# The final norm inside the last expert's block, and the last expert's rows added and stored behind it

## The reference

```
h = h + expert_choice_ffn(rmsnorm(h, ffn_norm))
    aff = softmax(t @ w_router)              # 16 experts
    g, idx = top_k(aff.T, 130)               # each expert takes 130 tokens of a group
    y = (silu(xs @ w_gate) * (xs @ w_up)) @ w_down * g
    out[idx] += y                            # a token may be taken by several experts or by none
h = rmsnorm(h, final_norm)
y = h[:, 16:]                                # without the meta tokens
```

## Time and profile before

| | |
|---|---|
| median of 3 runs | 3084.68 us (3084.18 to 3085.31) |
| the profiled execution's own time | 3086.83 us |
| its span | 3084.8 us |
| TensorE busy (matmuls) | 2849.3 us, 92% |
| VectorE, ScalarE, POOL busy | 1842.3 us (60%), 1484.3 us (48%), 664.6 us (22%) |
| mean granted clock of TensorE | 0.962 |
| moved by DMA | 475.79 MB, 154 GB/s |

### The profile page before, as it was taken

One profiled execution on the slowest core, in us unless ns is written; L12 is line 12 of the kernel. 1 busy time (PEld: TensorE's weight loads), 2 busy tenths in 40 slices (PEclk: granted clock), 3 DMA queues, 4 the chain that ended last, 5 costly groups with the idle time before them and its releaser, 6 DMA issues. The chain is left out here.

```text
span 3084.8 us, 56350 instructions
## 1 busy us (share of the span) xinstructions
PE 2849.3 (92%) x20020; PEld 2636.1 (85%) x20020; DVE 1842.3 (60%) x3159; ACT 1484.3 (48%) x2690; POOL 664.6 (22%) x1233
## 2 busy tenths in 40 slices
PE   8999687999999999999999999999955999999991
PEld 7888576999998888888899999988835999999990
DVE  6887555888887777677333343433354555556544
ACT  4333223888887777677322222321222445544532
POOL 0000000444444333333100000000021333333320
PEclk9999898999999999999999999999977999999995
DMA  6656599022022233442847575456644889888857
GB/s 217 178 170 193 164 285 271 21 70 70 22 52 74 73 89 84 112 115 74 256 122 227 140 213 148 137 172 205 186 139 113 204 204 208 204 200 201 200 112 246
DMA packets 596447, 475.79 MB, mean 154 GB/s; under 512 B 56640, under 2 KB 536560, under 8 KB 596288
## 3 DMA queue, kind: packets, MB, share of 16 engines
q1 hardware_dynamic: 577904, 439.28, 50.6%
q0 software_dynamic: 12288, 34.10, 6.2%
q10 hardware_dynamic: 6096, 0.40, 0.1%
HBM read 320.05 MB, written 153.62 MB: 154 GB/s over the span
## 5 line engine op out<-in xcount | busy, mean ns | idle before, releaser
L1444 DVE TENSOR_REDUCE t_peak<-t_s_ps 128x1 f32<-128x1024 f32 (+2 forms) x276 | 336.6, 1220 | 85.0 <-PE t_s_ps L1257 84.3
L1257 PE MATMUL t_s_ps<-t_k,t_q 96*128 96x512 f32 (+2 forms) x1392 | 380.1, 403 | 7.4 <-ACT t_probs L1360 7.4
L1705 PE MATMUL c_acc<-c_tokens,c_w_hi 128*128 128x260 f32 x2048 | 374.0, 284 | 5.3 <-DVE c_w_lo L1778 4.9
L1466 DVE TENSOR_TENSOR t_pt_lo<-t_tp,t_pt_hi 128x512 fp32r<-128x512 f32 x552 | 336.0, 649 | 32.6 <-ACT t_pt_hi L1390 32.1
L1390 ACT CAST t_pt_hi<-t_tp 128x512 fp32r<-128x512 f32 x552 | 284.6, 564 | 113.7 <-PE t_tp L1287 112.5
L1705 PEld LDWEIGHTS c_acc<-c_tokens,c_w_hi 128*128 128x128 f32 x2048 | 317.5, 189 | 5.6 <-issue 5.6
L1360 ACT ACTIVATE t_probs<-t_s_ps,t_bias 128x1024 f32<-128x1024 f32 (+2 forms) x276 | 308.2, 1117 | 22.8 <-POOL t_bias L1520 8.1
L2270 PE MATMUL e_gu<-e_x_hi,w_hi 128*128 128x260 f32 x1024 | 294.1, 287 | 0.9 <-DVE e_x_lo L2413 0.9
L1257 PEld LDWEIGHTS t_s_ps<-t_k,t_q 96*128 96x128 f32 (+2 forms) x1392 | 245.0, 183 | 53.0 <-issue 8.1
L1705 PE MATMUL c_acc<-c_tokens,c_w_lo 128*128 128x260 f32 x1024 | 290.2, 283 | 0.0
L2270 PE MATMUL e_gu<-e_x_lo,w_hi 128*128 128x260 f32 x1024 | 290.1, 283 | 0.0
(11 more groups left out here) (236 smaller groups left out, 6450.5 us busy)
## 6 DMA issues: line engine op xcount, KB each, us to landing
c_raw<-in_w_in SPq DMA_DIRECT2D x64, 512.0 KB, 5.5
w_raw<-in_w_gate SPq DMA_DIRECT2D x64, 512.0 KB, 6.6
w_raw<-in_w_up SPq DMA_DIRECT2D x64, 512.0 KB, 8.2
w_raw<-in_w_down SPq DMA_DIRECT2D x64, 512.0 KB, 4.6
c_tokens<-o_t SPq DMA_DIRECT2D x32, 520.0 KB, 6.7
c_tokens<-hn_t SPq DMA_DIRECT2D x16, 1040.0 KB, 9.1
r_mt<-mix_t SPq DMA_DIRECT2D x32, 512.0 KB, 5.1
t_k<-mk_t SPq DMA_DIRECT2D x32, 390.0 KB, 6.1
```

The costliest lines, as they stand in the source:

```text
L1257: ins = pe.matmul(s_ps[0:r, n % 2, half * 512:(half + 1) * 512], query(n, a), key(n, c, half * 512, (half + 1) * 512), start=(at == 0), st ...
L1444: dve.tensor_reduce(peak[0:r, b % 2, i:i + 1], s_ps[0:r, n % 2, :], AX_X, ALU.max).then_inc(peak_done, 1)
L1466: dve.tensor_tensor(pt_lo[span], tp[:, f % RING, :].rearrange("p (t n) -> p t n", t=4)[:, :, 0:r], pt_hi[span].bitcast(F32), ALU.subtract) ...
L1705: pe.matmul(acc[:, b, mixer, 0:W], w[:, parity, mixer, k, :], tokens[t % 2][:, part, k, cols], start=(k == 0 and at == 0), stop=(k == DK - ...
```

## The change

`finish` is gone, and its work stands in `experts`.

- **The split of results.** For expert 14 all four quarters are transposed at the beginning of the last expert (`results_alternating`), by turns into `tp` and `dn`, and scaled at once. POOL then scatters each quarter when it is done, not all four at the end.
- **The rows.** SP waits for that scatter and for the last weight slab to be split, then loads the 16 blocks of h into room that the weights no longer need (6 on `w_raw`, 4 on `w_hi`, 3 on `w_lo`) and 3 blocks of its own. The last expert's lists of ScalarE and VectorE are written out by hand (`last_body`): squares (L2469) and products (L2577, in place) stand between the `hidden` and `transposed` steps. The products are on VectorE alone. Roots are made in batches of four. SP stores each block as it is done.
- **The last expert's own rows.** POOL gathers their old values from `h_rows` (L2671). TensorE transposes expert 15's outputs into all eight banks; VectorE makes old + gate x output (L2611), ScalarE squares the 260 rows, VectorE makes the roots and the products (L2616), and POOL, once all 16 stores have landed, writes the rows over those stored (L2679). Row numbers of meta tokens lie beyond the bound and are not written.
- **Elsewhere.** `choose` makes the output row numbers `out_rows` (two small VectorE instructions). The gain is loaded on SP's queue as the first thing in `experts`. The weight tensors are now views of one region, at the same sizes. The bodies of experts 0 to 14 are the same but for the order of two waits on POOL.

```diff
-def choose(nc, io, scr, rows_t, gates_t, w_raw, w_hi, w_lo):
+def choose(nc, io, scr, rows_t, gates_t, out_rows, w_raw, w_hi, w_lo):
...
+            for g in range(GROUPS):
+                last = g * E + E - 1
+                dve.tensor_scalar(out_rows[:, :, g:g + 1], rows_f[:, :, last:last + 1], -float(g * SEQ), None, ALU.add)\
+                    .then_inc(done, 1)
...
-def experts(nc, io, scr, rows_t, gates_t, raw, w_hi, w_lo):
+def experts(nc, io, scr, outs, rows_t, gates_t, out_rows, weights, raw, w_hi, w_lo):
...
+        N = GROUPS * XCH
+        hi_at, lo_at = RAW * SLAB, RAW * SLAB + SLABS * SLAB
+        on_raw = weights.at(0, "f_on_raw", [P, 6, D])
+        on_hi = weights.at(hi_at, "f_on_hi", [P, 4, D])
+        on_lo = weights.at(lo_at, "f_on_lo", [P, 3, D])
+        unused = weights.at(lo_at + 3 * D, "f_unused", [P, D])
+        own = sb("own", [P, 3, D])
+        final_gain = sb("final_gain", [P, D])
+        homes = [on_raw[:, i, :] for i in range(6)] + [own[:, i, :] for i in range(3)] \
+            + [on_hi[:, i, :] for i in range(4)] + [on_lo[:, i, :] for i in range(3)]
+        mean, rs = sb("mean", [P, N + NT]), sb("rs", [P, 3, N + NT])
+        BATCHES = [(0, 4), (4, 8), (8, 12), (12, N), (N, N + NT)]
+        sum_banks = [tp[:, :, :], dn[:, :, :], gu[:, 0, :, :], gu[:, 1, :, :]]
+        gain_loaded, row_loaded, row_squared, root_chain, marked = (
+            sem("gain_loaded"), [sem(f"row_loaded{n}") for n in range(N)], sem("row_squared"), sem("root_chain"), sem("marked"))
+        row_done, row_stored = sem("row_done"), sem("row_stored")
+        old_gathered, sums_filled, sums_done, fixed, fix_stored = (
+            sem("old_gathered"), sem("sums_filled"), sem("sums_done"), sem("fixed"), sem("fix_stored"))
...
+            sp.dma_start(final_gain[:, :], spread(io["final_norm"], 0, P)).then_inc(gain_loaded, 16)
             body(1)
             with sp.Fori(2, E) as e:
                 body(e)
+
+            sp.wait_ge(scattered, 16 * NT * (E - 1))
+            sp.wait_ge(slab_lo, slab_number(E - 1, SLABS))
+            for n in range(N):
+                if n == 9:
+                    sp.wait_ge(gu_filled, FK * (E - 1) + 2)
+                sp.dma_start(homes[n], scr["h_rows"][n * P:(n + 1) * P, :]).then_inc(row_loaded[n], 16)
+            for n in range(N):
+                sp.wait_ge(row_done, n + 1)
+                sp.dma_start(outs[n // XCH][0, (n % XCH) * P:(n % XCH + 1) * P, :], homes[n]).then_inc(row_stored, 16)
+            sp.wait_ge(row_stored, 16 * N)
...
+                if is_last(e):
+                    results_alternating(e - 1)
...
+            def results_alternating(e):
+
+                pe.wait_ge(y_t_act, DK // 2 * (e + 1))
+                pe.wait_ge(y_t_dve, DK // 2 * (e + 1))
+                pe.wait_ge(x_hi_done, DK * (e + 2))
+                pe.wait_ge(x_lo_done, DK * (e + 2))
+                for t in range(NT):
+                    for half in range(2):
+                        pe.wait_ge(y_act if half == 0 else y_dve, NT * e + max(t - 1, 0))
+                        for k in range(4):
+                            ins = pe.transpose((tp, dn)[t % 2][0:HALF_CAP, half, k * P:(k + 1) * P],
+                                               y_t[:, half * 4 + k, t * HALF_CAP:(t + 1) * HALF_CAP], ident[:, :])
+                        ins.then_inc(y_filled, 1)
...
+                if is_last(e):
+                    pe.wait_ge(y_act, NT * e)
+                    pe.wait_ge(y_dve, NT * e)
...
+            pe.wait_ge(y_act, NT * (E - 1))
+            pe.wait_ge(y_dve, NT * (E - 1))
+            pe.wait_ge(h_done, FK * E)
+            pe.wait_ge(y_t_act, DK // 2 * E)
+            pe.wait_ge(y_t_dve, DK // 2 * E)
             for t in range(NT):
-                results_of(E - 1, t)
+                for k in range(DK):
+                    ins = pe.transpose(sum_banks[t][0:HALF_CAP, k // 4, k % 4 * P:(k % 4 + 1) * P],
+                                       y_t[:, k, t * HALF_CAP:(t + 1) * HALF_CAP], ident[:, :])
+                ins.then_inc(sums_filled, 1)
...
+            def square(lo, hi):
+                for n in range(lo, hi):
+                    act.wait_ge(row_loaded[n], 16)
+                    if n == 0:
+                        act.wait_ge(gu_filled, FK * (E - 1) + 2)
+                    at_least(act, row_squared, n)
+                    act.activation(unused[:, :], homes[n], ACT.Square, scale=D ** -0.5,
+                                   accum_out=mean[:, n:n + 1]).then_inc(row_squared, 1)
+
+            def square_sum(t):
+                act.wait_ge(sums_done, t + 1)
+                act.wait_ge(marked, 1)
+                act.wait_ge(row_squared, N + t)
+                act.activation(unused[0:HALF_CAP, :], y[:, t, :], ACT.Square, scale=D ** -0.5,
+                               accum_out=mean[0:HALF_CAP, N + t:N + t + 1]).then_inc(row_squared, 1)
+
+            def last_body(e):
+                for t in range(NT):
+                    results(e - 1, t, (tp, dn)[t % 2])
+                hidden(e, 0)
+                hidden(e, 1)
+                square(0, 3)
+                hidden(e, 2)
+                square(3, 7)
+                hidden(e, 3)
+                square(7, 9)
+                transposed(e, 0)
+                square(9, 11)
+                transposed(e, 2)
+                square(11, 13)
+                transposed(e, 4)
+                square(13, 14)
+                transposed(e, 6)
+                square(14, 16)
+                for t in range(NT):
+                    square_sum(t)
...
-            each_expert(dve, body)
-            gates_of(E - 1)
-            for t in range(NT):
-                results(E - 1, t)
+            def roots(i):
+                lo, hi = BATCHES[i]
+                link = Chain(dve, root_chain, RSQRT_OPS, i)
+                dve.wait_ge(row_squared, hi)
+                rsqrt(dve, link, rs[:, 0, lo:hi], mean[:, lo:hi], rs[:, 1, lo:hi], rs[:, 2, lo:hi])
+                link.end()
+
+            def normed(*rows):
+                for n in rows:
+                    dve.scalar_tensor_tensor(homes[n], homes[n], rs[:, 1, n:n + 1], final_gain[:, :],
+                                             ALU.mult, ALU.mult).then_inc(row_done, 1)
+
+            def last_body(e):
+                gates_of(e - 1)
+                for t in range(NT):
+                    results(e - 1, t, (tp, dn)[t % 2])
+                hidden(e, 0)
+                dve.memset(mean[:, N:], 1.0).then_inc(marked, 1)
+                dve.wait_ge(gain_loaded, 16)
+                hidden(e, 1)
+                hidden(e, 2)
+                roots(0)
+                normed(0)
+                hidden(e, 3)
+                normed(1, 2)
+                transposed(e, 1)
+                roots(1)
+                transposed(e, 3)
+                normed(3, 4)
+                transposed(e, 5)
+                normed(5)
+                gates_of(e)
+                transposed(e, 7)
+                normed(6, 7)
+                roots(2)
+                normed(8, 9, 10, 11)
+                roots(3)
+                normed(12, 13, 14, 15)
+                dve.wait_ge(old_gathered, 16 * NT)
+                for t in range(NT):
+                    dve.wait_ge(sums_filled, t + 1)
+                    if t == 0:
+                        dve.wait_ge(scattered, 16 * NT * e)
+                    dve.scalar_tensor_tensor(y[:, t, :], sum_banks[t][0:HALF_CAP, :, :].rearrange("p a b -> p (a b)"),
+                                             gates_now[:, t % 2, t // 2:t // 2 + 1], gathered[:, t, :],
+                                             ALU.mult, ALU.add).then_inc(sums_done, 1)
+                roots(4)
+                for t in range(NT):
+                    dve.scalar_tensor_tensor(y[:, t, :], y[:, t, :], rs[0:HALF_CAP, 1, N + t:N + t + 1], final_gain[0:HALF_CAP, :],
+                                             ALU.mult, ALU.mult).then_inc(fixed, 1)
+
+            body(0)
+            with dve.Fori(1, E - 1) as e:
+                body(e)
+            last_body(E - 1)
...
-                wait_alone(pool, y_act, NT * (e + 1), pool_passed)
-                wait_alone(pool, y_dve, NT * (e + 1), pool_passed)
                 wait_alone(pool, out_rows_copied, e + 1, pool_passed)
+                each = isinstance(e, int) and e == E - 2
                 for t in range(NT):
+                    if t == 0 or each:
+                        wait_alone(pool, y_act, NT * e + (t + 1 if each else NT), pool_passed)
+                        wait_alone(pool, y_dve, NT * e + (t + 1 if each else NT), pool_passed)
...
-            scatter(E - 1)
-
-            pool.wait_ge(scattered, 16 * NT * E)
...
+            wait_alone(pool, scattered, 16 * NT * (E - 1), pool_passed)
+            wait_alone(pool, x_filled, DK * E, pool_passed)
+            wait_alone(pool, row_loaded[N - 1], 16, pool_passed)
+            for t in range(NT):
```

(26 more changed lines are left out.)

88 lines of the change are left out of this document (21 added, 67 removed).

## The result

The changed kernel takes 3058.7 us (median of 4 runs, 3056.51 to 3061.68) beside 3084.99 us for the kernel before (4 runs, 3084.18 to 3088.23): ratio 0.9915, 95% interval 0.9903 to 0.9927, 26 us less. The forecast was 3070.0 (3063 to 3077): the direction was right, the gain nearly twice as large. The profiled execution spans 3055.0 us (its run 3056.82).

The account below looks back on a forecast made before the run. TensorE was taken to bound the kernel until 3011, then transfers. Steps to 3067.9, plus 0.4 and 1.2 at the experts' start and 0.8 for the clock, gave 3070.3 against 3084.8: -14.5, so 3070 from the median; range 3063.0 to 3077.0.

Parts of the forecast that it names:

- rival 2: VectorE's back-to-back products let no indirect transfer of POOL in; gather 12.2 us late, end 3084.1, no change; chance 0.05.
- Rival 3: TensorE stays at half clock through the last expert; +20.6 us, end 3090.8, slower than before; chance 0.02.
- rival 4: Misplaced scheduling: ScalarE later than set, or slower landings beside the stores; up to 3079; chance 0.08.
- From the last issue to the end: Kernel's end, waiting and DRAIN behind POOL's last scatter issue: 12.8 us as before, from 3055.1 to 3067.9.
- the nearer row is the one with scatters ahead of it: POOL's DRAIN at the end: between 0.04 and 5.78 us, taken as the long one seen behind scatters.
- Rival 1: No DRAIN at the end, the 5.78 us belonging to that one barrier; end 5.7 us sooner, 3064.5; chance 0.15.
- Three more issues at 2.05: POOL's last scatters: after the first, three more issues at 2.05 us each, the last at 3055.1.
- the extra waits that were put at 0.3 us: Scatter 14's issues: two more waits for each, not in the trace, between 0 and 0.6 us, taken as 0.3.
- the start of the experts: Two small VectorE instructions, 0.4 us, and the gain's load pushing back the first gather, 1.2 us (bounds 0 and 2).
- POOL starts 0.95 us after the first product: Last scatter's start: POOL begins 0.95 us after the first product of expert 15's rows, at 3047.9.
- The hold: Last scatter held by VectorE products with two SBUF inputs; 1.0 us taken, bounds 0.3 and 2.7.
- The clock: TensorE's granted clock falling low after the last expert's second thin stretch; 0.8 us taken, bounds 0 and 1.5.

Follow-up runs that it names:

- add_last: The changed kernel with its last four scatters adding in memory to the stored rows instead of replacing them; one run, 3069.81 us.

## Why the prediction was right or wrong

*Right: the direction and the mechanism.* The loads, squares and products went under the last expert, and the end became VectorE's queue: 16.9 us forecast from the last copy to the last outer product, 16.75 measured. Expert 14's results took what was said (0.1 us off), and POOL's gather of the old rows was hidden: rival 2 (VectorE locks POOL out) did not occur, the gathers were issued between 3013.4 and 3018.8, each held for less than 0.5 us. Rival 3 (half clock throughout) did not occur either; the clock fell for one stretch in half of the profiles. Nor did rival 4.

*Wrong: "From the last issue to the end", 12.8 us, measured 5.6.* This step is most of the miss, 7.2 us. "I take it again whole" overlooked that the change turns adding scatters into plain ones, which land 2.7 us earlier (3.9 instead of 6.6; add_last gives them back). And the DRAIN, "the nearer row is the one with scatters ahead of it", was tied to the wrong thing: not scatters ahead but the number of transfers decides, 128 before and 132 after. Rival 1 was nearly right by luck: it took 5.7 us off where 4.4 went, and for another reason. Its ground, "only one such DRAIN is in the trace", is misread as well: `choose` ends with a POOL DRAIN of 6.33 us (L2058, from 2313.4), but there POOL was still at its last subtraction, until 2319.6. Both numbers of the kernel before lay at hand, but one DRAIN of each kind cannot tell a cause.

*Wrong: "Three more issues at 2.05", measured 1.23* (2.33 behind the held one, then 1.24 and 1.22). Again the price of adding, 0.53 us each, and the extra waits that were put at 0.3 us cost nothing, in scatter 14 (issues every 1.76 us, as before) as here: 2.4 us together.

*Wrong by little:* the loads, the landing and ScalarE's turn came 2.5 us earlier than set (0.9 from the waits at 0.3, the rest from landings); the start of the experts cost 0.5 us instead of 1.6 (`choose` 46.86 us long instead of 46.71, from there to TensorE's first transpose 16.12 instead of 15.79, so the gain's load was mostly hidden). In the other direction, "POOL starts 0.95 us after the first product" was 2.4: the row behind it is that of a 121st transfer, and this is the 129th. The hold, taken as 1.0 with bounds 0.3 and 2.7, was 1.1.

*The clock*, 0.8 us with an upper bound of 1.5, turned out to be 0 or about 3. In the profile here it was 0.

*The range* reached down to 3063.0 with rival 1. It did not take in that landings and issues of a plain scatter could be cheaper, since the sum had no bounds on either; with 2.4 and 2.7 us below it would have reached 3058. Its lower end is also narrower than its own terms: all of them at their lower bounds (3066.7) and rival 1's 5.7 us together give 3061.0.

## What to carry to other kernels

When a change alters the kind of a transfer (here adding to replacing), price its issue, its landing and the queue's end anew; an adding indirect scatter of 65 rows cost 0.5 us more to issue and some 2 us more to land. Work moved under another stage is worth its whole length only where the engine that then sets the pace has room for it: here that was VectorE's order, and putting TensorE's needs first lost 4.4 us (one run). And look at what a barrier really waits for: of 5.8 us in one, 4.7 went away with one more transfer. Before a delay is put down to a pause, number the instructions: here the count, and not the pause, went with both odd times.
